# Two layers of a hybrid diffusion trunk on one core: regrouping the token tiles of merge and expert routing, and folding the norm vectors into the modulation rows

## The reference, cut to what matters

```
mod  = silu(cond) @ w_mod + b_mod          # 6 rows of 1024: sh1 sc1 g1 sh2 sc2 g2, one set for tile 0, one for tiles 1-4
h    = rmsnorm(x, g_attn_norm) * (1 + sc1) + sh1
mix  = (sum over 3 branches of sigmoid(h @ w_gate_b) * (branch_b @ w_o_b)) @ w_out     # "merge"
x    = x + g1 * mix
h    = rmsnorm(x, g_ffn_norm) * (1 + sc2) + sh2
q    = h @ w_pq ; top 16 of 128 keys, twice per head, for 8 heads                      # "route"
     ; top 16 of the 16 x 16 sums -> 128 (expert, gate) pairs per token                # "choose"
x    = x + g2 * sum over 128 slots of gate * gelu(u[expert] . h) * v[expert]           # "slots"
```

## Time and profile before

| | us |
|---|---|
| median of 3 runs | 5152.53 (5148.38 to 5156.72) |
| profiled execution, from first to last instruction (its span) | 5145.4 |
| PE busy | 3978.3 (77%) |
| DVE busy | 2905.9 (56%) |
| ACT busy | 1635.7 (32%) |
| POOL busy | 1556.1 (30%) |
| moved by DMA | 1640.19 MB, mean 319 GB/s |

### The profile page before, as it was taken

One profiled execution on the slowest core, in us unless ns is written; L12 is line 12 of the kernel. 1 busy time (PEld: TensorE's weight loads), 2 busy tenths in 40 slices (PEclk: granted clock), 3 DMA queues, 4 the chain that ended last, 5 costly groups with the idle time before them and its releaser, 6 DMA issues.

```text
span 5145.4 us, 62465 instructions
## 1 busy us (share of the span) xinstructions
PE 3978.3 (77%) x20366; PEld 1626.3 (32%) x20366; DVE 2905.9 (56%) x6315; ACT 1635.7 (32%) x4867; POOL 1556.1 (30%) x1453
## 2 busy tenths in 40 slices
PE   5988899778887666666679889997788887666666
PEld 3555653332223211111134556533322232111111
DVE  3543544675666676654445434446756667766544
ACT  0211542223333333333322115422233333333333
POOL 0210012233334444343312100132333344444432
PEclk8989999988999977666779899998889998677666
DMA  7126049899999999999941260498899999999998
GB/s 281 48 78 236 7 167 399 344 339 372 421 406 409 420 421 421 421 421 421 421 183 48 99 221 1 179 398 340 341 373 421 411 409 413 421 421 421 421 421 357
DMA packets 232449, 1640.19 MB, mean 319 GB/s; under 512 B 26688, under 2 KB 28864, under 8 KB 36800
## 3 DMA queue, kind: packets, MB, share of 16 engines
q0 software_dynamic: 184320, 1342.26, 63.8%
q1 hardware_dynamic: 47808, 293.94, 15.0%
HBM read 1632.82 MB, written 3.28 MB: 318 GB/s over the span
## 4 chain that ended last, share of the span: by engine, by line
PE 37%; DMA 35%; DVE 17%; issue 5%; ACT 4%; DVEq 2%; POOL 1%; SPq 0%; ACTq 0%; POOLq 0%
DMA arena<-in_experts,arena 30%; PE ps L751 12%; PE ps L985 8%; DVE sq L1455 6%; DMA front<-in_experts,arena 3%; PE ps L936 3%; PE ps L961 3%; DMA arena<-in_weights 2%; PE ps L888 2%; PE ps L949 2%; PE ps L913 2%; PE ps L900 1%; ACT arena L1122 1%; DVE arena L1185 1%; DVE negm L1346 1%
## 5 line engine op out<-in xcount | busy, mean ns | idle before, releaser
L985 PE MATMUL ps<-arena 64*64 64x512 f32 x9040 | 1569.3, 777 | 828.2 <-ACT arena L1122 813.5
L724 POOL DMA_INDIRECT arena<-in_experts,arena x1130 | 1261.1, 1116 | 2774.9 <-PE ps L985 1891.6
L1455 DVE CUSTOM_DVE_ANT_0 sq<-arena 128x1024 f32<-128x1024 f32 x1130 | 1386.1, 1227 | 909.4 <-DMA arena<-in_experts,arena 831.3
L985 PEld LDWEIGHTS ps<-arena 64*64 64x64 f32 x9040 | 312.8, 156 | 1923.1 <-issue 1900.5
L1116 ACT ACTIVATE arena<-arena 128x1 f32<-128x1 f32 x1280 | 258.4, 202 | 2073.9 <-DVE arena L1455 2058.2
L751 PE MATMUL ps<-arena 128*128 128x512 f32 (+3 forms) x1920 | 819.3, 574 | 21.9 <-DMA arena<-in_weights 20.0
L1122 ACT ACTIVATE arena<-ident,arena 128x128 f32<-128x128 f32 x1280 | 513.9, 402 | 91.8 <-issue 3.4
L751 PEld LDWEIGHTS ps<-arena 128*128 128x128 f32 x1920 | 360.3, 195 | 467.5 <-issue 427.0
L1118 ACT ACTIVATE arena<-arena 128x1 f32<-128x1 f32 x1280 | 376.7, 294 | 92.1 <-issue 5.2
L961 PE MATMUL ps<-arena 128*128 128x256 f32 (+1 forms) x1536 | 349.3, 372 | 6.3 <-issue 2.3
L961 PEld LDWEIGHTS ps<-arena 128*128 128x128 f32 x1536 | 251.7, 199 | 183.4 <-issue 150.5
(11 more groups left out here) (159 smaller groups left out, 3039.4 us busy)
## 6 DMA issues: line engine op xcount, KB each, us to landing
arena<-in_weights SPq DMA_DIRECT2D x242, 1024.0 KB
arena<-in_experts,arena POOLq DMA_INDIRECT x1130
arena<-mod_rows SPq DMA_DIRECT2D x24, 512.0 KB, 7.1
arena<-in_weights SPq DMA_DIRECT2D x8, 576.0 KB
arena<-in_keysT SPq DMA_DIRECT2D x4, 1024.0 KB, 12.9
arena<-in_g_norm SPq DMA_DIRECT2D x6, 512.0 KB, 9.4
arena<-in_weights SPq DMA_DIRECT2D x4, 768.0 KB
arena<-in_weights SPq DMA_DIRECT2D x6, 512.0 KB
```

The costliest lines, as they stand in the source:

```text
L724: pool.indirect_dma_start(out=ring[BUF[n]], out_offset=None, in_=ins["experts"], in_offset=bass.IndirectOffsetOnAxis(ap=index(t)[:, slot:s ...
L985: last = MM(acc[h][to:to + 64, c * 512:(c + 1) * 512], diag[n % 4][lo:lo + 64, lo:lo + 64], ring[BUF[n]][lo:lo + 64, D + c * 512:D + (c + ...
L1455: V.tensor_tensor_reduce(out=sq[:], in0=ring[BUF[n]][:, 0:D], in1=h2_of_slot(n), scale=1.0, scalar=0.0, op0=ALU.mult, op1=ALU.add, accum_o ...
```

## The change

Group 0 is now tiles 0 and 1, group 1 is tiles 2, 3 and 4, and there is no group 2. So attention of tiles 0 and 1 comes first, then merge and route of both with nothing else beside them, then attention of tiles 2 to 4 with `choose` of tile 0 among its 48 units. Under the slots `choose` of tile 1 lies over slots 8 to 100, merge and route of tiles 2 to 4 with `choose` of tile 2 over -3 to 248, `choose` of tile 3 over 258 to 340, of tile 4 over 350 to 450. Each layer now loads the 30 units of merge and route twice and not three times. `RELEASE` names items of group 1 in place of group 2.

The modulation multiplies the scale rows by the norm vector where they are computed, in 2x128 pieces, so the broadcast of the norm vector and the 128x1024 steps (L1284, L1385) are gone; four more small loads (`normrow`) come with `bmod`. `rows2` before group 0 now broadcasts both sets (6 rows), before group 1 one set again (3 rows). `index` and `gate` of every tile lie in its own `zt`. Some scratch places moved.

```diff
-GROUPS = {0: (0,), 1: (1, 2), 2: (3, 4)}
+GROUPS = {0: (0, 1), 1: (2, 3, 4)}
...
-        s += attention(l, (0,)) + [("rows2", l, 0), ("keys", l, 0)]
-        s += merge(l, 0) + route(l, 0) + [("sink", l, 1)]
-        s += attention(l, (1, 2, 3, 4), choose(l, 0)) + [("rows2", l, 1), ("keys", l, 1), ("g2", l, 0)]
+        s += attention(l, (0, 1)) + [("rows2", l, 0)]
+        s += merge(l, 0) + [("keys", l, 0)] + route(l, 0) + [("sink", l, 1)]
+        s += attention(l, (2, 3, 4), choose(l, 0)) + [("rows2", l, 1), ("keys", l, 1), ("g2", l, 0)]
...
-        line.spread(-3, 118, pieces(merge(l, 1) + route(l, 1, 1)))
-        line.spread(140, 236, choose(l, 2))
-        line.spread(118, 320, pieces(merge(l, 2) + route(l, 2)))
-        line.spread(322, 372, choose(l, 3))
+        line.spread(8, 100, choose(l, 1))
+        line.spread(-3, 248, pieces(merge(l, 1) + route(l, 1, 2)))
+        line.spread(258, 340, choose(l, 3))
...
-        line.spread(390, 490, choose(l, 4))
+        line.spread(350, 450, choose(l, 4))
...
-RELEASE = {6: lambda l: ("pq", l, 1, 15), 7: lambda l: ("pq", l, 2, 15), 8: lambda l: ("o", l, NT - 1, 1),
-           9: lambda l: ("sc", l, 2, 15), 10: lambda l: ("n2", l, NT - 1)}
+RELEASE = {6: lambda l: ("pq", l, 1, 15), 7: lambda l: ("pq", l, 1, 15), 8: lambda l: ("o", l, NT - 1, 1),
+           9: lambda l: ("sc", l, 1, 15), 10: lambda l: ("n2", l, NT - 1)}
...
+                        src = row("g_norm", l).rearrange("a (n g j) -> a n g j", g=4, j=P)[:, :, g, :].partition_broadcast(2).rearrange("p a n j -> p (a n) j")
+                        sp.dma_start(arena[32 * g:32 * g + 2, 1536:2048].rearrange("p (n j) -> p n j", j=P), src).then_inc(bmod_in, 16)
...
-                    sp.dma_start(grow1, to_all(row("g_norm", l)[:, 0:D])).then_inc(rows1_in, 16)
...
+                    for copy, who in ((2, 1),) if c else ((0, 0), (1, 1)):
+                        for j, k in enumerate((2, 4, 3)):
+                            sp.dma_start(rows2[copy][j], to_all(modd[l][who:who + 1, k * D:(k + 1) * D])).then_inc(rows2_in, 16)
...
+                    elif c in (1, 4):
+                        dve.drain()
+                        for g in range(4):
+                            row = modrow(c, g)[:, b % 2 * P:(b % 2 + 1) * P]
+                            last = STT(row, row, 1.0, normrow(c, g)[:, b % 2 * P:(b % 2 + 1) * P], ALU.add, ALU.mult)
...
-                        for c in range(2):
-                            STT(scale1[c], scale1[c], 1.0, grow1, ALU.add, ALU.mult)
...
-                        STT(rows2[t][1], rows2[t][1], 1.0, gnorm[t], ALU.add, ALU.mult)
```

More of the change, by code:

```diff
@@ L442 @@
 for _e, (_l, _t) in enumerate(ETILES):
-    if _t >= 3:
-        assert PLACE[("tk2", _l, _t, 0, 0)] > PLACE[("Emm", SLOTS * (_e - 1) - 1)]
     assert PLACE[("tkg", _l, _t)] < PLACE[("E", SLOTS * _e)]
@@ L507, in build @@
         modrow = lambda c, g: arena[32 * g:32 * g + 2, 256 * c:256 * (c + 1)]
+        normrow = lambda c, g: arena[32 * g:32 * g + 2, 1536 + 256 * (c // 4):1792 + 256 * (c // 4)]
         rsx = lambda m: scr(512 * m, 512)
@@ L517, in build @@
         oT = lambda t: zt(t)[:, 0:1536].rearrange("p (k n) -> p k n", k=12)
[L519 to L525, removed]
+        merged = lambda t: scr(D * t, D) if t < 2 else ar(HT0 + D, D) if t == 4 else at(8192 + D * (t - 2), D)
+        sg = lambda j, t: scr(2048 + 512 * (j % 2), 512) if t < 2 else at(18432 + 512 * (j % 2), 512)
+        pqb = lambda gid, q: scr(2048 + 256 * (q % 2), 256) if gid == 0 else at(17408 + 384 * (q % 2), 384)
+        scb = lambda gid, q: scr(2560 + 256 * (q % 2), 256) if gid == 0 else at(18176 + 384 * (q % 2), 384)
+        rows2 = [[a(D * j, D) for j in range(3)] for a in (lambda i, n: at(13442 + i, n), lambda i, n: scr(3072 + i, n), lambda i, n: at(12288 + i, n))]
+        keys = [a.rearrange("p (q n) -> p q n", q=16) for a in (scr(0, 2048), at(15360, 2048))]
         g2 = at(19456, D)
@@ L528, in build @@
         diag = [at(21504 + P * r, P) for r in range(4)]
-        index = lambda t: (zt(0)[:, 1536:1664] if t == 0 else at(22016 + P * (t % 2), P)).bitcast(U32)
-        gate = lambda t: zt(0)[:, 1664:1792] if t == 0 else at(22272 + P * (t % 2), P)
+        index = lambda t: zt(t)[:, 1536:1664].bitcast(U32)
+        gate = lambda t: zt(t)[:, 1664:1792]
         h2 = lambda t: zt(t)[:, 0:D]
@@ L656, in _ @@
                     sp.wait_ge(mod_stored[1], 64 * (l + 1))
[L657 to L660, removed]
+                    sp.wait_ge(*ready("om", l, (1, NT - 1)[c], 1))
+                    for copy, who in ((2, 1),) if c else ((0, 0), (1, 1)):
+                        for j, k in enumerate((2, 4, 3)):
+                            sp.dma_start(rows2[copy][j], to_all(modd[l][who:who + 1, k * D:(k + 1) * D])).then_inc(rows2_in, 16)
                 elif kind == "g2":
@@ L681, in _ @@
                 elif kind == "keys":
+                    if item[2] == 0:
+                        sp.wait_ge(*full("o", l, 1, 1))
                     sp.dma_start(keys[item[2]], row("keysT", l).rearrange("a p q n -> (a p) q n")).then_inc(keys_in, 16)
@@ L876, in _ @@
                             pe.wait_ge(*ready("sink", l, 0))
-                        elif (t, m) == (1, 1):
+                        elif (t, m) == (2, 1):
                             pe.wait_ge(*ready("sink", l, 1))
@@ L1220, in _ @@
                     if b == 0:
-                        dve.wait_ge(bmod_in, 64 * (l + 1))
+                        dve.wait_ge(bmod_in, 128 * (l + 1))
                     dve.wait_ge(*full(*item))
@@ L1382, in _ @@
                     t, c = item[2:]
-                    if t < 2 and c == 0:
-                        dve.wait_ge(rows2_in, 64 * (2 * l + t + 1))
-                        STT(rows2[t][1], rows2[t][1], 1.0, gnorm[t], ALU.add, ALU.mult)
-                        dve.drain()
+                    if t in (0, 2) and c == 0:
+                        dve.wait_ge(rows2_in, 144 * l + (144 if t else 96))
                     dve.wait_ge(*full(*item))
-                    done(TT(sq[:, 0:512], psum(item), rows2[min(t, 1)][0][:, c * 512:(c + 1) * 512], ALU.mult))
+                    done(TT(sq[:, 0:512], psum(item), rows2[min(t, 2)][0][:, c * 512:(c + 1) * 512], ALU.mult))
                     dve.drain()
@@ L1398, in _ @@
                     root()
-                    STT(h2(t), x[:, t, :], r1[:], rows2[min(t, 1)][1], ALU.mult, ALU.mult)
+                    STT(h2(t), x[:, t, :], r1[:], rows2[min(t, 2)][1], ALU.mult, ALU.mult)
                     dve.drain()
-                    done(TT(h2(t), h2(t), rows2[min(t, 1)][2], ALU.add))
+                    done(TT(h2(t), h2(t), rows2[min(t, 2)][2], ALU.add))
                     dve.drain()
```

10 lines of the change are left out of this document (2 added, 8 removed).

## The result

The changed kernel takes 5188.9 us (median of 4 runs, 5186.81 to 5189.86); the kernel before, run beside it, 5153.48. The ratio is 1.0076, 95% interval 1.0062 to 1.009: slower by 0.8%, where 5134 us and "faster" were forecast. Its profiled execution has a span of 5185.0 us, against 5145.4.

A forecast was written before the change was run, and what follows sets the result against it. It took DMA to bound most slots, DVE the first route and PE the front. Front +97, slots -105 and layer 1's fold -2.4 gave -8 and -10 us, a 5127 us span, 5134 with 7.1 on top; range 5055 to 5205.

The forecast's parts named there:

- The front: Work before slot 0, bound by PE: taking in tile 1 was to add 97 us per layer.
- +61.8: Front, `g` and `p` of tile 1: six blocks at 10.30 us each, +61.8 us per layer.
- -1.2: Front, joint of `p` and `o`: transposes of tile 0 lie in PE's wait for the last sum, -1.2 us.
- -7.2: Front: the 3.73 us wait for a gate unit goes and two gate products leave the lower clock, -7.2 us.
- Attention: Attention before slot 0: 24 `tk2` among 48 units, 0 to +4 us; one more `tk1` before its first maximum, +1.9.
- The fold: Norm vectors folded into the modulation: -2.4 us at layer 1's start; 0 (-2 to +4) in layer 0.
- The merge under the slots: Slots 0 to 138, three tiles: DMA the bound, PE close below, 418 us plus 8 for three `n2`, together 426.
- The route under the slots: 110 slots to 248: DVE and DMA equal, waits for scores on top; 325 us, between 294 and 339.
- the tail: The 71 slots from 248 to 320, with `choose` of tile 3: 2.52 us each, 179 us.
- rival 2: DVE and in-order joints hold slots 0 to 319 up: route 348 us, merge 440, total 5208; chance 0.27.
- break-even of 939 us: Rival 2's deciding time for slots 0 to 319: from 939 us on, the change loses.
- Rival 1: DMA stays full through merge and route: slots 0 to 319 take 900 us, total 5074; chance 0.30.

The follow-up runs named there:

- Experiment 7: The kernel before with only the norm vectors folded into the modulation's scales, old groups kept; 5138.12 us, 0.9982 of before.
- experiment 1: The changed kernel with every `tk1` of the route under the slots placed one q later than its `sc`; 5098.31 us, 0.9903 of before.
- experiment 2: The changed kernel with every second `pq` product left out for the group under the slots; 5154.79 us, 1.0014 of before.
- experiment 3: The changed kernel with each slot's second part (`Emm`) laid 2.6 slots after its first instead of 1.6; 5095.99 us, 0.9889 of before.
- experiment 5: The changed kernel with `tk1` one q later under the slots and the planner's costs set near traced durations; 5138.22 us, 0.9974 of before.

## Why the prediction was wrong

Its steps, in its order.

- **The front (+97): right within some 6 us.** Measured +100.0 and +99.3 for the whole stage before slot 0. Counted from the first product of attention to slot 0 it is +103.4 and +102.4; the stage before attention was 3.4 and 3.1 us shorter, in layer 1 by the fold, in layer 0 for a reason that no run shows apart (its length differs by up to 4 us between the traces). `g` and `p` of one block now take 20.6 us for both tiles, as forecast. From the first gate product to `o` it is 126.8 us (414.58 to 541.33) for 74.9: +51.9, where +61.8, -1.2 and -7.2 make +53.4. The -7.2 was read in layer 1; in layer 0 the same wait and the two slow products were 8.8 us, which is the difference.

```profile
414.58 7.03 PE L749 MATMUL ps<-arena 128*128 128x512 f32 x16
421.45 3.60 PE L934 MATMUL ps<-arena 128*128 128x512 f32 x8
...
541.33 27.63 PE L947 MATMUL ps<-arena 128*128 128x512 f32 x64
...
582.38 9.30 PE L959 MATMUL ps<-arena 128*128 128x256 f32 x32 [1.16 <-issue]
591.52 0.61 PE L967 MATMUL ps<-arena 128*128 128x128 f32 x4
592.16 3.72 PE L959 MATMUL ps<-arena 128*128 128x256 f32 x16
```

  The first gate product runs at 7.03 us, and none waits for weights. `o` to `pq` is +15.3 (forecast +15.6). The route is +29.3 for +26: a pair takes 4.2 us, not 4.0 (592.16 is 9.78 after 582.38 for two `pq` and a `sc`, the ones after it 4.19 apart).
- **Attention (0 to +4, with +1.9 for a `tk1`): a little short.** +6.9 together in layer 0 (255.2 us before, 262.1 after, from its first product to slot 0 without merge and route). The start of its second part has one new wait, 5.27 us for ACT at 661.81, while DVE is still in four `tk1`.

```profile
661.81 1.51 PE L898 MATMUL ps<-ident,arena 128*128 128x128 f32 x6 [5.27 <-ACT arena L1067]
```

- **The fold (-2.4 in layer 1, 0 in layer 0): under-sized.** Experiment 7 gives -6.5 in front of layer 1 and some -9 in all by the medians.
- **The merge under the slots (426 us to slot 138): right, in part by luck.** 426.4 us. But slots 0 to 128 take 379.2 us, 2.96 each where 3.03 were summed, and the end of the merge with its three `n2`, slots 128 to 140, takes 49.9 us for 12 slots, some 14 above that rate where 8 were allowed. The two errors cancel.
- **The route under the slots (325 us between 294 and 339): this is the step that failed.** Of its terms, the work of DVE was right. DMA's was small: 294 us for 124 MB, while the window moved 129 MB (356.3 us at 361 GB/s), 306 us at the forecast's 421 GB/s, and 312.6 in experiment 1 at 413. A part of that was missing from the tail, which moved 70 MB for 72 slots (their gathers are 75.5) and took 168.6 us for 179. But 306 is still 50 us below what was measured. The forecast had 292 us of DVE work; taking DVE's waits for scores and rows from the window leaves 356.3 - 60.7 - 7.2 = 288.4 after, 312.6 - 24.4 = 288.2 in experiment 1, 336.0 - 35.2 - 13.0 = 287.8 in experiment 2 and 314.8 - 11.6 - 15.5 = 287.7 in experiment 3. In these four windows the time is DVE's 288 us (its short gaps counted as work) and what it waits for. The waits were the error: 33 us allowed, 68 measured (61 for scores), outside even the upper bound of 339. The text scaled the 22 us of the earlier trace rows with the slots, to 47, and then took some off, because eight buffers would absorb it. But a buffer absorbs nothing of a wait between engines: the rows of the next slots had landed (7 us of waiting for them), and it was DVE that did not come to them. And the wait grew by more than the slots. A turn now holds three `tk1` on one side and 50% more of `pq` and `sc` on the other; that this is why it grew to 61 and not 47 is argued, though experiment 2, with half the `pq`, brought it to 35. The rate in the window, 361 and 351 GB/s, and 61 and 64 us of waiting for scores, are the signs that rival 2 named (under 365, over 40).
- **Rival 2** thus had the mechanism (route 348, 5208 in all) and a chance of 0.27. Its 348 is close by other terms, 301 and 47, than the measured 288 and 68. It was too dark on the merge (440 us), and its break-even of 939 us proved right: 954 and 957 lost, 937 and 934 in experiment 2 gave 1.0014, 913 and 908 won. **Rival 1** (DMA full throughout, 900 us for slots 0 to 319, 5074) is what the kernel comes close to once the order is mended: 907 and 900 us for the slots, 5092 in all. By the spans the two are 22 us apart (5088.6 against 5074 less the 7.1 of the forecast): 7 us in the slots of layer 0, and 15 in the front, +108 and +98 in that kernel for the forecast's +97 and +95.
- **The sum.** Forecast per layer +97 - 105 (-2.4) = -8 and -10; measured +100 - 82 - 2 = +16 in layer 0, and +99 - 77 + 2 = +24 in layer 1. Slots beyond 320 kept their rate, as forecast (-2.5 and +1.9 us). The miss of 24 us in layer 0 is the route's +34 and the front's +3, less 10 in the tail and 2.5 beyond slot 320.

On "DMA: Bandwidth & Descriptors", section Specifications, of the Trainium skill, with its 358 GB/s: the stages after run at 415 GB/s for 168.6 us, so the measurement again decides for this kernel, which runs on one core alone. What two cores together would get no run here shows.

What stays open: where the fold's 4 us under the slots of layer 0 come from, and whether a due time between those of experiments 1 and 5 would give both the merge at 299 us and the route at 304; no kernel here tried it.

## What to carry to other kernels

When a group of work grows, ask of each in-order queue how far apart in the list a step and the step that feeds it on another engine stand, not only how much each engine has to do: here all engines had room (DVE 70% busy, PE 73%, DMA at 93%), and two neighbours in the list cost 61 us of waiting per layer; moving one of them by one step took 44 and 49 us off the stage. A wait in the trace of before between two engines that ask for each other's newest result need not scale with the share of the work (here 47 us by the share, 61 measured); test the order by itself before the change is judged, since the same change was 0.8% slower with the old order and 1.1% faster with a better one. Then give the old kernel the same order before the gain is put down to the change: 0.7 of the 1.1% was there too. And of two gains that trade places, front for slots, 235 us against 215, the net of 21 us is small enough that an error of a tenth in either decides the sign.

## What the runs showed that I had not expected

- The lag between the two parts of a slot, which looks like a matter of buffers, is worth 1.9% in one kernel and 0.4% in another: in the changed kernel it keeps PE from standing before a slot whose dot product DVE has not begun.
- DVE's work in the route came to 287.7 to 288.4 us in four kernels with routes between 313 and 356 us. The same work with its small gaps took the same time in four orders; busy time alone (251 us) leaves out 37 us of it.
- Better costs made the plan worse (0.9903 to 0.9974): an error in a cost can be the slack of the stage that needs it most.
